# A mixture-of-experts stage without dense experts: tokens are sorted into slots ahead of the expert routing, and the modulated rows are no longer split

## What is computed

```python
x = x + mod_l[5] * hier_moe(modulate(rmsnorm(x, norm2_w[l]), mod_l[3], mod_l[4]), lp)

def hier_moe(h, lp):                       # t: 256 tokens x 1024
    g_logits = t @ moe_rg_w + moe_rg_b                    # 4 groups
    p_top, g_sel = top_k(softmax(g_logits), 1)            # one group per token
    e_logits = (t @ moe_re_w + moe_re_b)                  # 16 experts, 4 per group
    e_top, e_sel = top_k(e_logits of the picked group, 2) # two experts in it
    w_sel = p_top * softmax(e_top)
    a = silu(t @ moe_w_gate[e]) * (t @ moe_w_up[e]) * combine   # hidden width 256
    return sum over e of a @ moe_w_down[e]
```

## Time and profile before

| | |
|---|---|
| median of 3 runs | 2202.6 us (2197.62 to 2204.48) |
| profiled execution | 2202.33 us |
| its span | 2200.5 us |
| mean granted TensorE clock | 0.968 |
| TensorE busy (matmuls) | 94% |
| TensorE weight loads busy | 75% |
| VectorE / ScalarE / GpSimd busy | 60% / 44% / 5% |
| DMA queue with the weight stream | 349.20 MB, 43.5% of 16 engines |

### The profile page before, as it was taken

One profiled execution on the slowest core, in us unless ns is written; L12 is line 12 of the kernel. 1 busy time (PEld: TensorE's weight loads), 2 busy tenths in 40 slices (PEclk: granted clock), 3 DMA queues, 4 the chain that ended last, 5 costly groups with the idle time before them and its releaser, 6 DMA issues.

```text
span 2200.5 us, 27794 instructions
## 1 busy us (share of the span) xinstructions
PE 2068.6 (94%) x11292; PEld 1657.7 (75%) x11292; DVE 1317.7 (60%) x1936; ACT 961.9 (44%) x1534; POOL 120.6 (5%) x120
## 2 busy tenths in 40 slices
PE   6999899998999988999999998999998999989997
PEld 2468667766788676887899986888896888857886
DVE  3355823235888675554777785655776655747554
ACT  2233431004788464444454553544464444454442
POOL 1000000000100020000001112000011000020000
PEclk8999999998999989999999998999999999989999
DMA  8142453533789533545443432555433555424451
GB/s 345 55 157 83 161 199 128 188 147 111 270 320 345 192 105 135 189 176 190 169 163 134 149 133 94 195 182 182 172 135 139 186 189 175 157 83 161 184 187 62
DMA packets 48895, 370.08 MB, mean 168 GB/s; under 512 B 5578, under 2 KB 5749, under 8 KB 9920
## 3 DMA queue, kind: packets, MB, share of 16 engines
q1 hardware_dynamic: 43632, 349.20, 43.5%
q0 software_dynamic: 4848, 18.64, 2.5%
q10 hardware_dynamic: 288, 0.47, 0.1%
HBM read 367.23 MB, written 1.05 MB: 167 GB/s over the span
## 4 chain that ended last, share of the span: by engine, by line
PE 85%; DVE 9%; ACT 4%; issue 1%; DMA 1%; POOL 0%; SPq 0%; ACTq 0%; DVEq 0%
PE pg L485 54%; PE pd L485 26%; PE pm L485 3%; PE pm L1089 1%; DVE small L2218 1%; DVE rs L2254 1%; DMA ring<-in_wstream 1%; DVE low L1908 1%; DVE rs L2253 1%; DVE rs L2214 1%; PE pm L1229 1%; DVE ar L2012 1%; ACT high L1362 1%; ACT ar L1794 1%; DVE xs L2264 1%
## 5 line engine op out<-in xcount | busy, mean ns | idle before, releaser
L1908 DVE TENSOR_TENSOR low<-ring,high 128x1024 fp32r<-128x1024 f32 x536 | 644.6, 1230 | 299.6 <-ACT high L1362 298.6
L1362 ACT CAST high<-ring 128x1024 fp32r<-128x1024 f32 x536 | 547.3, 1048 | 301.7 <-PE pd L485 122.0
L485 PE MATMUL pg<-high,xs 128*128 128x512 f32 (+1 forms) x2048 | 600.9, 372 | 22.4 <-DVE xs L2264 13.2
L485 PEld LDWEIGHTS pg<-high,xs 128*128 128x128 f32 x2048 | 377.6, 194 | 92.3 <-issue 21.2
L485 PE MATMUL pg<-low,xs 128*128 128x512 f32 (+1 forms) x1024 | 378.0, 369 | 0.0
L485 PE MATMUL pd<-high,hid 128*128 128x512 f32 x880 | 287.3, 396 | 5.6 <-DVE hid L2379 5.6
L485 PE MATMUL pg<-xs,high 128*128 128x256 f32 x1344 | 242.1, 283 | 0.0
L485 PEld LDWEIGHTS pg<-low,xs 128*128 128x128 f32 x1024 | 198.8, 194 | 31.0
L485 PEld LDWEIGHTS pg<-xs,high 128*128 128x128 f32 x1344 | 206.1, 188 | 5.3 <-issue 5.0
L485 PE MATMUL pg<-rh,ring 128*128 128x256 f32 (+1 forms) x832 | 206.5, 408 | 0.0
L485 PEld LDWEIGHTS pd<-high,hid 128*128 128x128 f32 x880 | 165.6, 188 | 45.6 <-DVE hid L2379 6.6
(11 more groups left out here) (373 smaller groups left out, 2225.8 us busy)
## 6 DMA issues: line engine op xcount, KB each, us to landing
ring<-in_wstream SPq DMA_DIRECT2D x208, 1024.0 KB, 4.8
ring<-in_wstream SPq DMA_DIRECT2D x31, 2048.0 KB, 7.8
ring<-in_experts SPq DMA_DIRECT2D x60, 1024.0 KB, 4.8
gb<-in_long_rows POOLq DMA_DIRECT2D x21, 512.0 KB, 4.6
hdec<-in_hy_decay POOLq DMA_DIRECT2D x4, 512.0 KB, 6.8
rh<-in_xt SPq DMA_DIRECT2D x1, 1024.0 KB, 11.7
rh<-in_ctx SPq DMA_DIRECT2D x1, 1024.0 KB, 19.9
cx<-in_cx_tables POOLq DMA_DIRECT2D x1, 1024.0 KB, 5.1
```

The lines of the kernel that those rows point to most:

```text
L485: ins = nc.tensor.matmul(dst, lhs, rhs, start=start, stop=stop, skip_group_check=skip)
L1362: nc.scalar.copy(high[:, (s - split0) % NHIGH, :], ring[:, s % NRAW, :]).then_inc(S("high_done"), 1)
L1908: V.tensor_tensor(low[:, s % NRAW, :], ring[:, s % NRAW, :], high[:, (s - split0) % NHIGH, :].bitcast(F32), ALU.subtract).then_inc(S("low_ ...
```

## The change

`DENSE` is gone: all 20 steps are block steps, with four experts in each of the five blocks (`block_of(u)` is `(u // 4, u % 4)`), and no step runs over 256 tokens. The modulated rows `h1` are only made for the logits; they are no longer copied to `xs` and no longer subtracted, and the waits for `x_high` and `x_ready` of this norm become waits for `h1_out`. On VectorE the sorting now stands right behind the logits of the picked group and ahead of the choice of experts; the one-hot of block 0 is signalled by itself (`first_hot`), then that of blocks 1 to 4 (`slots_hot`). TensorE gathers block 0 before any expert work; the shares' matmuls stand inside step 0. The weights of block 4's tokens are no longer a separate table. GpSimd's work on the dense output is gone. The reads of `DENSE` steps in the ScalarE, VectorE and TensorE programs are removed, and the gather of block 1 stands in step 2 (before: in step 3).

```diff
-DENSE = 2
 def block_of(u):
-    return (0, u) if u < 4 else (1 + (u - 4) // 4, u % 4)
+    return u // 4, u % 4
...
@@ GpSimd @@
-            gp.wait_ge(S("gains_landed"), 48)
-            for i, t in enumerate((1, 0)):
-                gp.wait_ge(S("y_out"), 2 * i + 2)
-                gp.tensor_tensor(y_dense[:, t, :], y_dense[:, t, :], gb[:, 1, :], ALU.mult).then_inc(S("dense_added"), 1)
-                gp.wait_ge(S("dense_added"), 2 * i + 1)
-                gp.tensor_tensor(x[:, t, :], x[:, t, :], y_dense[:, t, :], ALU.add).then_inc(S("dense_added"), 1)
...
@@ TensorE: slot_shares, gather_block @@
-                pe.wait_ge(S("sorted"), SORTED["slots_hot"])
+                pe.wait_ge(S("sorted"), SORTED["shared"])
                 for b in range(BLOCKS):
-                    lo = 70 if b < BLOCKS - 1 else 122
...
-                if b == 0:
-                    pe.wait_ge(S("sorted"), SORTED["slots_hot"])
-                elif b == 1:
-                    pe.wait_ge(S("y_out"), 2)
-                else:
-                    pe.wait_ge(S("y_out"), 2 * b + 2)
+                pe.wait_ge(S("sorted"), SORTED["slots_hot" if b else "first_hot"])
+                if b == 1:
+                    pe.wait_ge(S("sorted"), SORTED["shares_out"])
+                elif b:
+                    pe.wait_ge(S("y_out"), 2 * b - 2)
...
@@ TensorE: experts @@
-                ffn_up(0, (0,))
                 logit_columns()
-                ffn_up(0, (1, 2))
                 rank_tokens()
-                ffn_up(0, (3,))
-                ffn_up(1, (0, 1))
-                turn_hidden(0)
-                ffn_up(1, (2,))
                 gather_block(0)
-                slot_shares()
-                ffn_up(1, (3,))
-                pe.wait_ge(S("xb_high"), 3)
-                pe.wait_ge(S("sorted"), SORTED["shares_out"])
-                ffn_down(0, (0, 1), True)
-                for u in range(DENSE, STEPS):
+                for u in range(STEPS):
                     b, j = block_of(u)
                     up_block(u, (0,))
-                    if u == DENSE:
-                        turn_hidden(u - 1)
-                    else:
+                    if u:
                         turn_block(u - 1)
                     up_block(u, (1,))
-                    if b < BLOCKS - 1 and j == (2 if b else 3):
+                    if u == 0:
+                        slot_shares()
+                    if b < BLOCKS - 1 and j == 2:
                         gather_block(b + 1)
                     if u == 6:
                         slot_rows()
                     up_block(u, (2, 3))
-                    if u == DENSE:
...
-                    else:
+                    if u:
                         down_block(u - 1)
...
@@ ScalarE: norm(1), then the routing and the steps @@
-                            then(last)
-                            src = h1[:, ks, tok]
+                            last.then_inc(S("h1_out"), 1)
...
+            split_to(split0 + 5)
             act.wait_ge(S("group_diff"), 1)
             nc.scalar.activation(route[:, 40:48], route[:, 40:48], ACT.Exp).then_inc(S("group_exp"), 1)
-            act.wait_ge(S("pair_diff"), 1)
-            nc.scalar.activation(route[:, 100:102], route[:, 100:102], ACT.Exp).then_inc(S("pair_exp"), 1)
...
+            take_block(0)
+            act.wait_ge(S("pair_diff"), 1)
+            nc.scalar.activation(route[:, 100:102], route[:, 100:102], ACT.Exp).then_inc(S("pair_exp"), 1)
             experts_act()
...
@@ VectorE: norm, sorting ahead of the choice of experts @@
-            low_part(1, 0)
             normalised(1, 1)
-            low_part(1, 1)
...
+            then(V.tensor_tensor(named, oh3, group_id.unsqueeze(1).to_broadcast([P, 2, 4]), ALU.mult))
+            then(V.tensor_reduce(grp, named, AX, ALU.add))
+            V.tensor_scalar(shift, grp, -float(P), float(3 * P), ALU.mult, ALU.add)
+            dve.wait_ge(S("sorting"), SORTING["ranked"])
+            then(V.tensor_tensor(picked, oh3, pm[1][:, 0:8].rearrange("p (s c) -> p s c", s=2), ALU.mult))
+            then(V.tensor_reduce(rnk, picked, AX, ALU.add))
+            V.tensor_scalar(beyond, rnk, P - 0.5, None, ALU.is_gt)
+            then(V.scalar_tensor_tensor(slot, grp, float(P), rnk, ALU.mult, ALU.add))
+            then(V.tensor_tensor(shift, shift, beyond, ALU.mult))
+            then(V.tensor_tensor(slot, slot, shift, ALU.add))
+            then(V.tensor_tensor(in_block, slot.unsqueeze(2).to_broadcast([P, TT, BLOCKS]),
+                                 block_lo.unsqueeze(1).to_broadcast([P, TT, BLOCKS]), ALU.subtract))
+            def hot_slots(lo, n):
+                for t in range(TT):
+                    last = V.tensor_tensor(slot_hot[:, t, lo:lo + n, :], iota.unsqueeze(1).to_broadcast([P, n, P]),
+                                           in_block[:, t, lo:lo + n].unsqueeze(2).to_broadcast([P, n, P]), ALU.is_equal)
+                last.then_inc(S("sorted"), 1)
+            hot_slots(0, 1)
+            hot_slots(1, BLOCKS - 1)
...
             V.tensor_tensor(pdiff, m2, m1, ALU.subtract).then_inc(S("pair_diff"), 1)
+            lower_block(0)
             dve.wait_ge(S("group_exp"), 1)
...
+            V.tensor_tensor(o1, o1, o2, ALU.add).then_inc(S("sorted"), 1)
...
@@ VectorE: experts_hidden @@
-                for u in range(DENSE, STEPS):
+                for u in range(STEPS):
                     b, j = block_of(u)
-                    split_to(UP[u] + 7)
-                    if u == DENSE:
-                        hidden_low(u - 1)
+                    split_to(UP[u] + (7 if u else 5))
+                    if u == 0:
+                        dve.wait_ge(S("sorting"), SORTING["shares_done"])
+                        V.tensor_copy(share_of, pd[:, 2, 0:20]).then_inc(S("sorted"), 1)
+                        dve.wait_ge(S("sorted"), SORTED["shares_out"])
                     else:
                         block_low(u - 1)
```

More of the change, by code:

```diff
@@ L975, in up_block @@
                 for i in parts:
-                    if i == 0:
-                        pe.wait_ge(S("h_raw"), 2 * (u - 1) + int(u == 2))
+                    if i == 0 and u >= 2:
+                        pe.wait_ge(S("h_raw"), 2 * (u - 1))
                     if i % 2 == 0:
@@ L1051, in experts @@
                     up_block(u, (2, 3))
-                    if u == DENSE:
-                        pe.wait_ge(S("hid_ready"), u)
-                        for i in range(2):
-                            for t in range(TT):
-                                for h in range(2):
-                                    last = down_part(u - 1, i, t, h, False, True)
-                            last.then_inc(S("unit_used"), 1)
-                    else:
+                    if u:
                         down_block(u - 1)
@@ L1688, in take_block @@
                     nc.scalar.copy(xb[:, b % 2, 0, 4 * h:4 * h + 4, :], hb[h]).then_inc(S("xb_high"), 1)
-            def take_dense():
-                act.wait_ge(S("unit_used"), DOWN[DENSE - 1] + 2 - split0)
-                for t in (1, 0):
-                    for h in range(2):
-                        nc.scalar.copy(y_dense[:, t, h * 512:(h + 1) * 512], pd[:, 2 * t + h, :]).then_inc(S("y_out"), 1)
             def take_output(b):
-                last = (3, 7, 11, 15, 19)[b]
-                act.wait_ge(S("unit_used"), DOWN[last] + 2 - split0)
+                act.wait_ge(S("unit_used"), DOWN[4 * b + 3] + 2 - split0)
                 for h in range(2):
@@ L2319, in _ @@
                     then(V.tensor_tensor(ein, ein, etmp, ALU.add))
+            slot, rnk, grp, beyond, shift = (sort[:, 2 * i:2 * i + 2] for i in range(5))
+            picked, named = (sort[:, 16 + 8 * i:24 + 8 * i].rearrange("p (s c) -> p s c", s=2) for i in range(2))
+            in_block = sort[:, 32:42].rearrange("p (t b) -> p t b", t=TT)
+            busy, over = sort[0:1, 48:52], sort[0:1, 52:53]
+            then(V.tensor_tensor(named, oh3, group_id.unsqueeze(1).to_broadcast([P, 2, 4]), ALU.mult))
@@ new lines, in _, with lower_block @@
+            hot_slots(0, 1)
+            hot_slots(1, BLOCKS - 1)
+            then(V.tensor_scalar(busy, pm[1][0:1, 8:12], P + 0.5, None, ALU.is_gt))
+            then(V.tensor_tensor(busy, busy, group_id[0:1, :], ALU.mult))
+            then(V.tensor_reduce(over, busy, AX, ALU.add))
+            V.tensor_copy(over_int[0:1, :], over).then_inc(S("sorted"), 1)
+            def lower_block(b):
+                for h in range(2):
+                    dve.wait_ge(S("xb_high"), 4 * b + 2 * h + 2)
+                    ks = slice(4 * h, 4 * h + 4)
+                    V.tensor_tensor(xb[:, b % 2, 1, ks, :], hb[h], xb[:, b % 2, 0, ks, :].bitcast(F32), ALU.subtract
+                                    ).then_inc(S("xb_ready"), 1)
@@ L2335, in _ @@
             then(V.tensor_tensor(o2, o2, wide(w2), ALU.mult))
-            then(V.tensor_tensor(o1, o1, o2, ALU.add))
```

(6 more changed lines are left out.)

111 lines of the change are left out of this document (22 added, 89 removed).

## The result

The changed kernel took 2185.19 us in the median of its runs (2183.06 to 2188.91), against 2203.34 for the kernel before on the same chip: a ratio of 0.9928 with a 95% interval of 0.9906 to 0.9949, 16 us by the ratio. The forecast was 2185.6, in a range of 2181 to 2193.

The account below looks back on a forecast made before the run. TensorE sets the pace, with the weight stream a close second. Terms up to the fifth step (566.2 instead of 583.25 us) sum to 17.0 us gained: 2202.6 - 17.0 = 2185.6 us, range 2181 to 2193.

Parts of the forecast that it names:

- Modulated rows: Norm ahead of the logits: without copies and subtractions the logits' matmuls start at 511.3 instead of 515.05, 3.75 us gained.
- The exposed routing: From the logit matmuls' end (513.25) to the first up matmul (525.8): 12.5 us in which before the dense expert ran.
- The waits in step 0: TensorE waits for VectorE in step 0: 1.0 us before the shares, 0.8 us before transposing its hidden rows.
- Steps 1 to 3 and all behind: Steps of 8.54 us, plus a 3.57 gather in step 2; fifth step at 566.2 us, same work as before behind.
- Rival D: Weight stream takes gain back in the block steps: at most 1.5 us, 3 to 8 with late casts; chance 0.06.
- the rule against it: Behind 566.2 us steps need 368 GB/s; at the skill's 358 a step takes 8.79 and nineteen add 4.7 us.
- Rival B: First block rougher: longer low clock, or VectorE and ScalarE 2 to 3 us late; gain 9 to 14 us; chance 0.24.
- A: Whole kernel: the sum holds within 3 us, gain 14 to 20 us; chance 0.52.
- Rival E: Clock stays at 0.50 from 519 to 566 us, making the kernel slower, 2214 us; chance 0.03.
- Rival C: Clock up by the middle of the first gather, small operations overlap better: another 3 us, 2182 us; chance 0.12.
- The cross-check: Differences up to the fifth step: 26.2 us gained (1.3 the dense stage's leftover), 9.2 lost, the same 17.
- The signs: Places in the profile: gather at 519 to 520 us, clock 0.50 behind the shares; a gather after 521 would disprove the forecast.

Follow-up runs that it names:

- run 2: Changed kernel with the sorting moved back behind the choice of experts: gather at 19.55 us instead of 17.86, step 3's transposes at 68.25 instead of 66.67.
- run 11: The changed kernel measured again with no edit: median 2185.76 us, ratio 0.9924 to the kernel before.
- run 3: Changed kernel without the (low, high) product in all block matmuls: a block of four steps takes 35.1 to 35.7 us instead of 37.7.
- run 6: Changed kernel with units 4 to 7 split ahead of the logits and the shares behind step 0's up matmuls: step 3's transposes at 64.6 us.
- run 8: Changed kernel with early splits, shares behind step 0's up matmuls and 34 extra matmuls: median 2181.71 us, ratio 0.9915 to the kernel before.
- run 9: Kernel of run 8 with the shares in five groups among step 0's last 12 up matmuls and unit 7's cast later: 2178.6 us, ratio 0.9895.
- run 10: Kernel of run 9 without the extra matmuls: median 2181.88 us, ratio 0.9924 to the kernel before.

## Why the prediction was right, point by point

- **Modulated rows, 3.75.** Measured 4.3 in the profiles (13.0 to 8.7) and by putting them back. Of the 0.6 us more, 0.46 is that the second transposes took 0.67 us instead of the 1.13 of the earlier trace rows: they now stand earlier, ahead of the fall of the clock.
- **The exposed routing, 12.5 us from the end of the logit matmuls to the first up matmul.** Measured 14.0, from 513.8 (511.84 + 1.98) to 527.8. Two terms were mis-sized, in one way: I took the short matmuls at 0.107 us from a stretch with the full clock. At 0.50 the columns took 1.05 instead of 0.4 and the ranking 2.31 instead of 1.1, and VectorE waited 0.5 us for it, which the forecast had named as possible. That is 1.15 of the 1.5 us. The one-hot of the first block took 0.50 us until the gather was released, for 0.45. The gather took 6.13 instead of 5.47, since the clock came back later in it, but the first up matmul needs only its first half, which was 0.25 later than forecast (ScalarE starts 3.82 us behind the gather's start, for 3.57).
- **Order of the sorting.** Not a term of its own in the sum; run 2 gives 1.7 us for it at the gather, and leaves open what remains at the end.
- **The waits in step 0.** Before the shares 0.98, forecast 1.0. Before step 0's transposes 2.2, forecast 0.8; but the 1.65 us of slow matmuls behind the shares, charged ahead of that wait, did not occur in this profile. From the shares to those transposes it was 8.9 us for 8.8, and that the errors cancel is luck. Here VectorE's seven splits set the point, so quicker matmuls only waited longer. In run 11, the same kernel, the point comes 10.9 us behind the start of the shares: the shares 3.57 (2.15 in the sum, again at the price of the full clock), twelve matmuls 4.9, six more 1.4, and a wait of 1.0 that is not for the splits but for ScalarE's table load and activation. The sum had nothing for these two, only 0.5 for the hidden product.
- **Steps 1 to 3 and all behind.** 12.10, 8.51 and then 8.54 us a step, no gap. The second gather's new place, the removed copies and GpSimd's work, and SP's read of the group cost nothing that the chain shows.
- **Rival D and the rule against it.** The stream did not take anything back. These two stretches of the changed kernel (columns as in run 3) have the same pace as the earlier trace rows:

```profile
680.00:690.00 10.00, 10.00 (x46) 8.13 (x45) 9.24 (x11) 7.48 (x9) 0.00 (x0) 1.00 0.95 369
...
700.00:710.00 10.00, 10.00 (x47) 8.15 (x46) 9.29 (x11) 7.75 (x11) 0.00 (x0) 1.00 0.98 378
```

  The Trainium skill, HBM Reference (Specifications), says that a core alone goes well above its share of about 358 GB/s, and run 3's trace agrees: 403 for 10 us.
- **Rival B** was half true: the low clock covered more of the routing (the 1.15 us above), and VectorE was late with its units. In run 11, with the clock fallen behind the shares, the gain up to step 3 is 13.6 us, which is B's 9 to 14 and no longer A's. Rival E needed a low clock through steps 1 to 3; it was 1.00 there from step 0's transposes on in the changed kernel's two profiles. Rival C, a gain of 20, was not seen in the stage.
- **The sum.** 15.8 us in this profile and 13.6 in run 11's, for 17.0. The whole gained 16 by the ratio and 18 by the medians; what that is above the stage's own gain comes from parts that were not changed, and run 11 shows how much they vary. That the median came within 0.4 us of 2185.6 is therefore luck; the mechanism and a sum that is 1.2 to 3.4 us too large are what stands. The cross-check could not show it: it used the same 12.5 and the same waits, and its 1.3 was what was left over.
- **The signs.** From the first transposes the gather stands at 17.9 for 17.2. By the span's own time it stands at 521.03, past the 521 that was to prove the forecast wrong, because this execution reached the stage 1.1 us later. The clock did not fall behind the shares in this profile, and did in run 11.

## What to carry to other kernels

When work that covers a serial chain is removed, price the chain at the clock that the idle engine will have, not at the one of the trace: here the short matmuls doubled, which was 1.15 us in the columns and the ranking, and another 1.4 in the shares of run 11. Look next at who has a backlog when the cover ends; its idle time ahead of the chain is the place to work it off. A table load that stands on the chain is such a backlog too. And measure an edit of a few us by a place inside the profile, from an event that all versions share: the whole time of this kernel varied by more than the edits did.

## What was not expected of the hardware

- The shares in one piece (20 records of 4 columns, 2.4 us) left TensorE's clock at 0.50 behind them in seven profiles of the changed kernel and its edits and at 1.00 in four, with the same instructions in one pair of them (the changed kernel and run 11). In three of the seven (runs 2, 6 and 8) the shares themselves still ran at the full clock; in the other four it fell while they ran. In groups of four between matmuls of 512 columns it stayed at 1.00 both times (runs 9 and 10); two profiles do not exclude chance, since it also stayed up in four of eleven with the shares in one piece. The Trainium skill, TensorE: Matmul & The Clock Gate (Part 1), says that activity releases the low clock, and the changed kernel's gather shows it (0.50 in 522 to 524, 1.00 in 526 to 528). What this case adds is that the clock also falls where the profile shows TensorE busy: in run 8 there was no wait between the first up matmul (523.74) and the fall (0.89 in 530 to 532, 0.50 in 532 to 534).
- 34 matmuls with no purpose made the chain 3.6 us shorter up to the first up matmul: at 1.2 GHz, for all or part of their length, the gather, logits, columns and ranking together had cost 4.6 us more than at 2.4 (2.3, 0.9, 0.4 and 1.0).
- With a third of TensorE's work removed (run 3) a block of four steps gains 6%: the three limits of a block step lie that close together.
- A table load of ScalarE took 1.28 us. In run 11 it is more than half of the 2.4 us from the last up matmul of step 0 (539.1) to the transposes (541.48).
